# Block 0 of the output projection loaded in the last head's iteration, its units for six tiles first, and tiles turned back ahead of the next ones turned forth

## The reference

```python
h = concat(meta, x)
u = rms_norm(h, norm_mix); proj = u @ w_in
q, k, v = split(silu(causal_depthwise_conv(proj.qkv)))
o = chunk_gated_delta_rule(l2(q), l2(k), v, g, beta)     # a scan over chunks of tokens
y_a = rms(o) * head_norm * silu(z)
y_b = multiscale_causal_pool(proj.pool)
y = sigmoid(ga) * y_a + sigmoid(gb) * y_b
h = h + y @ w_out                                        # the output projection
f = rms_norm(h, norm_ffn) @ w_up; f = causal_depthwise_conv(f)
h = h + (silu(f.gate) * f.val) @ w_down
out = rms_norm(h, norm_final)[meta:]
```

## Time and profile before

| what | us |
|---|---|
| median of three runs (1749.07 to 1750.23) | 1749.51 |
| the profiled execution | 1749.15 |
| its span, first to last instruction | 1747.3 |
| PE busy in it | 1682.9 (96%) |
| DVE, ACT, POOL busy | 895.4, 609.7, 484.0 |
| mean granted clock of PE | 0.987 |

### The profile page before, as it was taken

The page is one execution under the profiler, slowest core; times in us unless marked ns, Lnnn a source line. Parts: engine busy times, 40 slices in busy tenths (PEclk is TensorE's granted clock), DMA queues, the critical chain, the costliest instruction groups (busy, mean ns, idle before and its releaser), DMA issues.

```text
span 1747.3 us, 30707 instructions
## 1 busy us (share of the span) xinstructions
PE 1682.9 (96%) x12131; PEld 1609.2 (92%) x12131; DVE 895.4 (51%) x971; ACT 609.7 (35%) x984; POOL 484.0 (28%) x469
## 2 busy tenths in 40 slices
PE   6999999997999999999789899999999999999997
PEld 6999999997999999999689898998998998989986
DVE  5566555484544454544441555545445456455447
ACT  6333465354444444443222531221212211212213
POOL 3222221136445444445011122212211221221210
PEclk9999999998999999999889999999999999999998
DMA  6223433348446445344871111111111111111112
GB/s 191 76 91 101 139 123 102 89 131 193 128 138 165 117 136 156 113 138 119 231 256 32 37 48 49 48 36 48 52 44 36 60 48 36 60 48 36 48 36 97
DMA packets 239654, 167.41 MB, mean 96 GB/s; under 512 B 43881, under 2 KB 225992, under 8 KB 238457
## 3 DMA queue, kind: packets, MB, share of 16 engines
q1 hardware_dynamic: 205492, 130.39, 26.2%
q10 hardware_dynamic: 33892, 36.28, 6.2%
q0 software_dynamic: 224, 0.12, 0.0%
HBM read 124.40 MB, written 42.37 MB: 95 GB/s over the span
## 4 chain that ended last, share of the span: by engine, by line
PE 87%; DVE 5%; DMA 2%; issue 2%; ACT 2%; POOLq 1%; DVEq 0%; POOL 0%; ACTq 0%; SPq 0%
PE gb L801 63%; PE db L1128 13%; PE db L938 4%; PE db L854 1%; PE db L1003 1%; PE db L1004 1%; DVE cacc L1604 1%; DMA ot_d<-ots 1%; DVE hx L1897 1%; PE db L1081 1%; PE db L935 1%; DVE fino L2003 1%; ACT hx L1175 0%; DVEq L1567 0%; DMA yo<-ot_d 0%
## 5 line engine op out<-in xcount | busy, mean ns | idle before, releaser
L801 PE MATMUL gb<-u_hi,w_hi 128*128 128x342 f32 (+2 forms) x2520 | 822.7, 326 | 20.3 <-ACT ht L1476 8.9
L801 PE MATMUL gb<-u_lo,w_hi 128*128 128x342 f32 (+2 forms) x2520 | 810.0, 321 | 0.0
L801 PE MATMUL gb<-u_hi,w_lo 128*128 128x342 f32 (+2 forms) x2520 | 806.8, 320 | 0.0
L688 POOL TENSOR_TENSOR w_lo<-w_raw,w_hi 128x1024 fp32r<-128x1024 f32 x127 | 322.7, 2545 | 1070.1 <-ACT w_hi L1170 1070.1
L801 PEld LDWEIGHTS gb<-u_hi,w_hi 128*128 128x128 f32 x2520 | 478.0, 190 | 24.9 <-issue 19.5
L801 PEld LDWEIGHTS gb<-u_lo,w_hi 128*128 128x128 f32 x2520 | 478.0, 190 | 0.4
L801 PEld LDWEIGHTS gb<-u_hi,w_lo 128*128 128x128 f32 x2520 | 477.4, 189 | 0.0
L1969 DVE TENSOR_TENSOR h<-h,db 128x512 f32<-128x512 f32 x176 | 117.0, 684 | 59.3 <-PE db L1128 58.8
L1128 PE MATMUL db<-w_hi,a_hi 128*128 128x512 f32 x352 | 140.9, 400 | 2.9 <-DVE a_lo L1993 2.9
L1128 PE MATMUL db<-w_lo,a_hi 128*128 128x512 f32 x352 | 139.6, 397 | 0.0
L1128 PE MATMUL db<-w_hi,a_lo 128*128 128x512 f32 x352 | 139.5, 396 | 0.0
(11 more groups left out here) (236 smaller groups left out, 1675.5 us busy)
## 6 DMA issues: line engine op xcount, KB each, us to landing
w_raw<-in_w_in SPq DMA_DIRECT2D x53, 512.0 KB, 4.0
w_raw<-in_w_up SPq DMA_DIRECT2D x44, 512.0 KB, 3.8
w_raw<-in_w_down SPq DMA_DIRECT2D x22, 512.0 KB, 3.3
qkT_d<-sl ACTq DMA_DIRECT2D x16, 576.0 KB, 2.8
kv_d<-tm ACTq DMA_DIRECT2D x16, 576.0 KB, 3.4
tk<-kv_d SPq DMA_DIRECT2D x9, 1024.0 KB, 7.7
kT<-qkT_d SPq DMA_DIRECT2D x9, 512.0 KB, 4.7
brow<-rows_d SPq DMA_DIRECT2D x9, 512.0 KB, 6.1
```

The source lines that it names most:

```text
L688: pool.tensor_tensor(lo, w_raw[:, n % SLOTS, :], hi.bitcast(F32), ALU.subtract).then_inc(s_wlo, 1)
L801: mm = pe.matmul(gb[:, bank, 0:w], wt, u, start=(k == 0 and m == 0), stop=(k == KT - 1 and m == 2))
```

## The change

Block 0 is loaded without the last head for `yz` and `yg` (7 of 8 tiles); for that head's part DVE reads the buffers `zs` and `gs` themselves. The waits of SP are loosened to match, and the tile of `ots` is put elsewhere, so that block 1's `yo` no longer waits for the write of the last OT. The weight tiles of `w_out` are loaded in the order `OUT_TILES`, tiles 0, 1 and 2 a second time. The plan begins with six tiles of block 0, with OT after two of them, then tiles 3 to 5 of blocks 1 and 2, and in its last part back stands ahead of forth. In the last down projection the first halves of eight outputs run ahead, in the four banks of `db`, three of `gb` and `mb`.

```diff
-W_UP0 = W_OUT + KT
+OUT_TILES = [0, 1, 2, 3, 4, 5, 0, 1, 2, 6, 7]
+W_UP0 = W_OUT + len(OUT_TILES)
...
-OUT_PLAN = [("unit", n, b) for b in range(3) for n in range(3)]
-OUT_PLAN += [("unit", n, b) for n in (3, 4) for b in range(3)]
-OUT_PLAN += [("unit", n, 0) for n in (5, 6, 7)]
-OUT_PLAN += [("unit", 5, 1), ("back", 0), ("unit", 6, 1), ("forth", 0), ("back", 1)]
-for _j, _unit in enumerate([("unit", 7, 1), ("unit", 5, 2), ("unit", 6, 2), ("unit", 7, 2), ("up", 0, 0),
+OUT_PLAN = [("unit", 0, 0), ("unit", 1, 0), ("OT",), ("unit", 2, 0)] + [("unit", n, b) for b in range(3) for n in (3, 4, 5)]
+OUT_PLAN += [("unit", n, b) for n, b in ((0, 1), (0, 2), (1, 1), (1, 2), (6, 0), (7, 0))]
+OUT_PLAN += [("unit", 2, 1), ("back", 0), ("unit", 6, 1), ("back", 1), ("forth", 0)]
+for _j, _unit in enumerate([("unit", 7, 1), ("unit", 2, 2), ("unit", 6, 2), ("unit", 7, 2), ("up", 0, 0),
                             ("up", 1, 0), ("up", 0, 1)]):
-    OUT_PLAN += [_unit, ("forth", _j + 1), ("back", _j + 2)]
+    OUT_PLAN += [_unit, ("back", _j + 2), ("forth", _j + 1)]
 OUT_PLAN += [("up", 1, 1), ("forth", KT), ("up", 0, 2), ("up", 1, 2)]
 OUT_UNITS = [s[1:] for s in OUT_PLAN if s[0] == "unit"]
 assert sorted(OUT_UNITS) == [(n, b) for n in range(KT) for b in range(3)]
+FIRST_OF_BLOCK = [(0, 0), (3, 1), (3, 2)]
+def out_slot(n, b):
+    return n if n in (3, 4, 5) or b == 0 and n < 3 else n + 6 if n < 3 else n + 3
+OUT_LAST = {out_slot(n, b): (n, b) for n, b in OUT_UNITS}
...
-        vv, vb, ots = plan(square_set("vv", "vb", "ots"), after_qkm)
+        vv, vb = plan(square_set("vv", "vb"), after_qkm)
+        (ots,) = plan(square_set("ots"), last_set + 4 * KT * TO)
...
+        def down_bank(u, last=False):
+            if not last or u % 8 < 4:
+                return db[:, u % 4, :]
+            return gb[:, u % 4, :] if u % 4 < 3 else mb[:, :]
...
-            for n in range(3):
-                load_w(W_OUT + n, cols(w_out, n * P))
+            def load_out(k):
+                load_w(W_OUT + k, cols(w_out, OUT_TILES[k] * P))
+            for k in range(3):
+                load_out(k)
             chunk_loads(NCH - 1, True)
...
-            def load_y(b, src, dst):
+            def load_y(b, src, dst, n=KT):
                 o, w = OBLOCKS[b]
-                sp.dma_start(dst[b % 2][:, :, :], src[:, o:o + w].rearrange("(k p) t -> p k t", p=P)
+                sp.dma_start(dst[b % 2][:, 0:n, :], src[0:n * P, o:o + w].rearrange("(k p) t -> p k t", p=P)
                              ).then_inc((s_ygin if dst is yg else s_yin)[b % 2], 16)
...
-            sp.wait_ge(s_za, 16 * HEADS)
+            sp.wait_ge(s_za, 16 * (HEADS - 1))
             sp.wait_ge(s_ps["QK"], 2 * NCH)
             sp.wait_ge(s_kg, NCH)
             sp.wait_ge(s_qd, NCH)
-            load_y(0, za_d, yz)
+            load_y(0, za_d, yz, HEADS - 1)
             sp.wait_ge(s_ev["QK"], 2 * NCH)
-            sp.wait_ge(s_ot, 16 * (NCH - 1))
+            sp.wait_ge(s_ot, 16 * (NCH - 2))
             load_y(0, ot_from, yo)
+            load_out(3)
             sp.wait_ge(s_rd, NCH)
             sp.wait_ge(s_ev["Y1"], 2 * (NCH - 1))
             sp.wait_ge(s_vb, NCH)
             sp.wait_ge(s_kd, NCH)
+            sp.wait_ge(s_yg, 16 * HEADS)
+            load_y(0, yg_d, yg, HEADS - 1)
+            load_out(4)
+            sp.wait_ge(s_ps["O"], 2 * NCH)
+            sp.wait_ge(s_za, 16 * HEADS)
+            load_y(1, za_d, yz)
             sp.wait_ge(s_yg, 16 * (HEADS + 1))
-            load_y(0, yg_d, yg)
-            sp.wait_ge(s_ps["O"], 2 * NCH)
-            load_y(1, za_d, yz)
             load_y(1, yg_d, yg)
+            load_out(5)
             sp.wait_ge(s_ps["OT"], 2 * NCH)
-            sp.wait_ge(s_ot, 16 * NCH)
             load_y(1, ot_from, yo)
-            load_w(W_OUT + 3, cols(w_out, 3 * P))
             sp.wait_ge(s_y, 2)
             load_y(2, za_d, yz)
             load_y(2, yg_d, yg)
+            sp.wait_ge(s_ot, 16 * NCH)
             load_y(2, ot_from, yo)
-            for n in (4, 5):
-                load_w(W_OUT + n, cols(w_out, n * P))
+            for k in (6, 7, 8):
+                load_out(k)
...
                 if g < 2:
-                    load_w(W_OUT + 6 + g, cols(w_out, (6 + g) * P))
+                    load_out(9 + g)
...
-            for name, prev in (("P1", LAST_Y), ("V", "P1"), ("O", "V"), ("OT", "O")):
-                step(name, NCH - 1, (prev, 2 * (NCH - 1)))
+            for name, prev in (("P1", TOP_X), ("V", LAST_Y), ("O", "P1")):
+                step(name, NCH - 1, (prev, 2 * (NCH - 2 if prev == TOP_X else NCH - 1)))
...
-                    w_ready(W_OUT + n)
+                    k = W_OUT + out_slot(n, b)
+                    w_ready(k)
                     pe.wait_ge(s_gfree, U_OUT - 3 + q + 1)
                     for hf in range(2):
-                        if n == 0:
+                        if (n, b) in FIRST_OF_BLOCK:
                             pe.wait_ge(s_y, 2 * b + hf + 1)
-                        mm = unit(W_OUT + n, q % 3, o, w, 4 * hf, 4 * hf + 4)
+                        mm = unit(k, q % 3, o, w, 4 * hf, 4 * hf + 4)
                     mm.then_inc(s_g, 1)
                     q += 1
+                elif kind == "OT":
+                    step("OT", NCH - 1, ("V", 2 * (NCH - 1)))
...
-                    mm = pe.matmul(db[:, u % 4, :], a, wt, start=(q == 0 and m == 0), stop=(q == 1 and m == 2))
+                    mm = pe.matmul(down_bank(u, n == W_LAST), a, wt, start=(q == 0 and m == 0), stop=(q == 1 and m == 2))
...
-            for u in range(4):
+            for u in range(KT):
+                if u == 4:
+                    pe.wait_ge(s_gfree, U_FFN + 12 * (FFN_ITERS - 1))
                 down_part(W_LAST, u, 0)
             for u in range(2 * KT):
                 if u % KT == 0:
                     pe.wait_ge(s_alo, FT + u // KT)
-                if u > 3:
-                    pe.wait_ge(s_dnfree, 16 * (FFN_ITERS - 1) + u - 3)
+                if u >= KT:
+                    pe.wait_ge(s_dnfree, 16 * (FFN_ITERS - 1) + u - KT + 1)
                     down_part(W_LAST, u, 0)
...
-            for name in REC:
-                act_step(name, NCH - 1)
...
+            act_step("V", NCH - 1)
             y_high(0)
+            act_step("O", NCH - 1)
+            act_step("SU", NCH - 1)
+            act.wait_ge(s_yg, 16 * (HEADS + 1))
...
-                if kind == "unit":
+                if kind == "OT":
+                    act_step("OT", NCH - 1)
...
-                    if n == 0 and b < 2:
+                    if n == 5 and b < 2:
                         y_high(b + 1)
...
-                    if b == 2:
-                        w_high(W_OUT + n + 3)
+                    if OUT_LAST[out_slot(n, b)] == (n, b):
+                        w_high(W_OUT + out_slot(n, b) + 3)
...
                 elif kind == "back":
-                    j = tile[0]
-                    n = HALO if j == 0 else P
-                    act.wait_ge(s_h2, 2 * j + 2)
...
-                    root(j, n, h2m[:, :] if j == 0 else h2[:, j - 1, :], hx[0:n, j % 2, :], s_h2sq)
+                    if tile[0] < 2:
+                        root2(tile[0])
                 else:
                     high2(tile[0])
+                    if 0 < tile[0] < KT:
+                        root2(tile[0] + 1)
...
-            def y_product(b):
+            def y_parts(b, kept, loaded):
+                o, w = OBLOCKS[b]
+                for ks in FEATURE_HALVES:
+                    if b or ks.stop < KT:
+                        yield ks, loaded[b % 2][:, ks, :]
+                    else:
+                        yield slice(ks.start, KT - 1), loaded[0][:, ks.start:KT - 1, :]
+                        yield slice(KT - 1, KT), kept[:, o:o + w].unsqueeze(1)
+            def y_low(b):
+                o, w = OBLOCKS[b]
                 s = b % 2
                 dve.wait_ge(s_yin[s], 32 * (b // 2 + 1))
...
-                    dve.tensor_tensor(yo[s][:, ks, :], yo[s][:, ks, :], yz[s][:, ks, :], ALU.mult)
-            dve_step("P1", NCH - 1, True)
-            y_product(0)
-            output_sums(NCH - 1)
-            output_scale(NCH - 1)
-            def y_low(b):
-                o, w = OBLOCKS[b]
-                s = b % 2
+                for ks, z in y_parts(b, zs, yz):
+                    dve.tensor_tensor(yo[s][:, ks, :], yo[s][:, ks, :], z, ALU.mult)
                 dve.wait_ge(s_ygin[s], 16 * (b // 2 + 1))
-                if b:
...
-                for ks in FEATURE_HALVES:
-                    dve.tensor_tensor(yo[s][:, ks, :], yo[s][:, ks, :], yg[s][:, ks, :], ALU.add).then_inc(s_y1, 1)
+                for ks, g in y_parts(b, gs, yg):
+                    t = dve.tensor_tensor(yo[s][:, ks, :], yo[s][:, ks, :], g, ALU.add)
+                    if ks.stop in (KT // 2, KT):
+                        t.then_inc(s_y1, 1)
...
-            for b in range(len(OBLOCKS)):
-                y_low(b)
+            dve_step("P1", NCH - 1, True)
```

(14 more changed lines are left out.)

17 lines of the change are left out of this document (11 added, 6 removed).

## The result

The changed kernel takes **1726.76 us** (median of four runs, 1724.27 to 1729.08) against 1749.29 (1748.84 to 1750.23): ratio 0.9875, 95% interval 0.9863 to 0.9888. The forecast was 1725.2, with a range from 1719 to 1735. Its profiled execution took 1727.12 us, span 1725.3, where the kernel before had 1747.3.

The account below looks back on a forecast made before the run. TensorE bounds the kernel nearly everywhere, so only its waits and low clock count. 19.0 - 0.9 - 0.3 + 5.0 + 1.5 = 24.3 us off 1749.15 gives 1724.9, as a median 1725.2 us, range 1719 to 1735.

Parts of the forecast that it names:

- Start of the first unit: Output projection, block 0: early loads end DVE's waits, so the first unit starts at 850.2 against 859.4.
- The clock behind that gap: Gap of 2.4 us before the first unit: a clock loss there only shortens the wait before block 2.
- Block 1: Output projection: yo lands 7.8 us after issue; PE may take the block at 874.5 to 875.3, waiting 0 to 1 us.
- Block 2 decides: Tenth unit: yo waits for OT's write, the row of loads takes 21 us, ready at 888.5; gain 19.0 us.
- The write of OT: Before block 2: earlier 11.1 us looked queued behind prior loads; by the packet-by-packet rule it would land early.
- Rival B: Before block 2: OT's write lands last, ready at 892.6, clock falls; +5, about 1730, up to 1734; chance 0.16.
- Rival A: Block 2 hidden too: loads at the full window's rate, PE waits under 1 us; about 1721; chance 0.15.
- C: Block 0's loads: held by a hidden wait, or they push bds back; at worst about 1738; chance 0.08.
- D: Gap before the first unit: clock falls and stays down, slower from 155 low matmuls on; up to 1756; chance 0.02.
- Turning phase: Back ahead of forth removes eight 0.34 us waits for hx and a low-clock unit; gain 5.0 us (2.5 to 5.4).
- a low clock behind block 2's gap: Output projection: a gap of 2.4 to 3.4 us costs 1.8 us about every second time; -0.9 (0 to 1.8).
- Last down projection: Kernel's end: 12 more matmuls fill the wait for a_lo, six behind run at full clock; gain 1.5 us (0 to 1.6).

Follow-up runs that it names:

- e6: Changed kernel, with POOL's split of the third weight tile held until DVE is through with block 0; 1725.10 us.
- e9: The changed kernel, unedited, timed and profiled a second time; 1726.05 us.
- e7: Changed kernel plus 14 idle matmuls in TensorE's gap between O and the first unit; 1724.61 us.
- e10: Changed kernel, with the sixth weight tile's load issued ahead of block 1's yz and yg instead of behind them; 1725.20 us.
- e1: Kernel before, with the new turning order alone (back ahead of forth, root and scaling placed to match); 1743.39 us.
- e2: Kernel before, with the new last down projection alone (eight first halves ahead instead of four); 1748.71 us.
- e3: Changed kernel, with turning order and last down projection put back, so the output projection's first-block change alone; 1731.65 us.
- e12: Changed kernel, with yz and yg of block 1 read from block 2's columns in memory and the reverse; 1731.41 us.
- e8: Changed kernel, with block 2's yz and yg loads held until the write of OT has landed; 1730.54 us.
- e5: Changed kernel, with the old order of three tiles per block and eight weight loads put back; 1737.14 us.

## Why the prediction was right, step by step

**Start of the first unit**: 850.2 forecast, 852.50 measured, 851.0 on the clock of the kernel before. That the loads would be there was right (DVE waits for none). The 0.8 us missing are DVE's product behind POOL's split (0.96 by e6). My price came from rows with POOL idle, and what POOL does beside them was no term of mine.

**The clock behind that gap**: I let it cost nothing, since the wait before block 2 would swallow it. The gap was 3.3 us instead of 2.4 and the first two units lost 1.6 us (2.7 in e9) against those of e7. It did pass into a later wait, as said, the one before block 1: 3.1 us in e7, 1.9 in the first profile, 0.4 in e9. But it also moved OT: PE came to it at 861.65, 1.6 us later than without the low clock (e7), and block 1's yo left as much later.

**Block 1**: "a wait of 0 to 1 us" was 1.9 and 0.4 in two profiles. The step that failed in the first is the landing time 7.8 us, which was 9.0 (7.2 in e9; 6.1 to 10.2 over all kernels): it was taken as a property of the load, and depends on how much of the row that began with block 1's yz is still under way.

**Block 2 decides**: the row of loads, 21 us from block 1's yo to block 2's, was 21.3 (862.71 to 884.0) and 19.7 in e9. That the first profile repeats the 21 us of the kernel before is luck in part: before, block 2's yo left 7.6 us behind block 1's and took 13.3; now it waited for the write of OT, left 12.7 us behind and took 8.6. Ready at 892.2 by DVE's row plus half of it, PE there at 892.5, so there was no wait to see: the forecast one of 2.4 to 3.4 us had been spent before, in front of the first unit and of block 1, together with the low clock (e9 has 0.64 us of it). Tenth unit: gain 19.0 forecast, 16.5 and 17.6 measured. The prediction's estimate by the memory limit in the Trainium skill ("DMA: Bandwidth & Descriptors", section Bandwidth) was 19.1 us for this row. The traces reach it in e10 (19.1), where the loads issued before the row had only 0.5 us left when it began, and not with more left of them: 19.7 in e9 (1.7 us left), 21.3 in the first profile (3.1), 21.8 in e7 (5.6). The limit itself, 358 GB/s, was passed a little: 364 GB/s from 864 to 880 us in the first profile.

**The write of OT**: 11.1 us again (10.4 in e9), but not as the earlier trace rows was read: it did not stand behind all that had been issued before it, and once it moved it took turns packet for packet, as the rule has it that the prediction takes from the Trainium skill ("DMA: Bandwidth & Descriptors", section Queues, rings and completion order). The row spoke against the rule only in the sum, since a start some 4 us late stands in it. Rival B came close to true in the first profile: block 2's yo left only at 875.40, when the write was in, and the block was ready at 892.2 (890.7 on the clock of the kernel before) against its 892.6; its low clock and its price of 5 us did not come, since PE was not there earlier. e9 (ready at 889.3, or 889.8 on that clock) lies nearer to the forecast 888.5. Rival A (block 2 hidden) is true in name, PE waited less than 1 us there, but the time went elsewhere. C and D fell: yz left 0.56 us behind bds, and behind the first gap some 12 matmuls ran low (20 in e9), not 155.

**Turning phase**: 5.0 forecast, 6.3 alone by the trace of e1 and 5.5 by its time. The small waits went for good. Seven of the eight cost 0.57 us, not 0.34: a forth that starts after a stop takes 1.09 us in the chain, one that runs behind back 0.87. That makes 4.3 us instead of 2.8. On the other side 1.5 us of the low clock were chance (paid in the kernel before and e2, not in e3). In the changed kernel the stage from the tenth unit on was 5.7 us shorter, and the forecast for it is 5.0 less the two terms that fall there: 0.9 for a low clock behind block 2's gap, which did not come (no gap, and 0.64 us at a granted clock of 1.00 in e9), and 0.3 for the last weight tile, which was 0.2. So 3.8 forecast.

**Last down projection**: 1.5 forecast, 1.3 by traces (1.0 to 2.2), below what the times can tell (e2).

So the sum was right within 1 us (23.5 and 24.6 for 24.3) with errors of opposite signs: 2.5 us too much to the tenth unit (1.4 in e9), 1.9 too little behind it. That they cancel is luck. What was right in the mechanism is which waits go, that the work put into them is what counts, and that block 2's last load stands behind the write; what was wrong is where PE would wait.

## What to carry to other kernels

Price a wait by what PE could do meanwhile, not only by how early its cause can be moved: the tiles put into the wait were worth 10 us, the early loads 6 to 7. Before moving one load, follow back the whole row of transfers in front of it, and ask what the second bound is, since here edits that each hit one of two gave at most 1 to 2 us at the load and nothing sure in the time. Compare short stages from a common late event: 1.5 us of difference in the spans arose more than 350 us ahead of the change.

## What the hardware showed that was not expected

**Columns of a matrix in memory load at different rates.** The same 128x8 rows of 1368 bytes, 4104 bytes apart, load at 229 GB/s from columns 342 to 683 and at 374 from 684 to 1025, in either order of time (e12), the engines full in both cases. The cause is open; yo, whose rows are farther apart (4608 bytes), loaded in company with the fast columns at 348 to 394 GB/s (windows of 2 us from 866 to 876 us in the changed kernel). Trying another row length for za and yg is the next thing to do here, and it was not done.

**POOL and DVE exclude each other, and who pays changes from profile to profile.** The changed kernel is 1.5 us late before its own change: up to 418 us it was 0.8 us early, and from that P1 to the next one, near 479, it lost 2.4. In this stretch one DVE instruction stands out; kernel before, then changed, timelines of DVE:

```profile
419.66 1.70 DVE L1673 TENSOR_TENSOR kgt<-kbt,grow 128x1024 f32<-128x1024 f32 x1
```

```profile
418.82 6.29 DVE L1711 TENSOR_TENSOR kgt<-kbt,grow 128x1024 f32<-128x1024 f32 x1
```

and the changed kernel's POOL in that stretch:

```profile
419.40 4.63 POOL L712 TENSOR_TENSOR w_lo<-w_raw,w_hi 128x1024 fp32r<-128x1024 f32 x2
```

In both kernels DVE's instruction began while POOL's product `kd` was under way (418.38 to 420.28 before, 417.55 to 419.44 after). Before, DVE got through in between, and POOL's two splits took 5.62 us. After, POOL went from `kd` into the first split and from that into the second, and DVE ended 1.1 us behind them. So in these rows DVE, though it waited, did not get in between POOL's instructions; that tenths of a microsecond decide it is my reading. PE's wait behind it was 8.10 us instead of 4.76. It is not the whole scatter: in eleven of the other twelve profiles the instruction took 1.70 us and in e8 3.00, and e2, e5 and e10, whose P1 comes as late or later (842.8 to 843.6), were late by 418 us already.

**The clock does not follow the length of the gap alone.** In the changed kernel and all that are built on it, the 4 us behind every gap of 1.82 to 12.10 us between the first unit and block 2 show a granted clock of 0.50 to 0.66, so TensorE ran at the lower of its two levels (1.2 GHz) for a part of them; behind gaps of 1.1 us and less they show 1.00. But in the turning phase a gap of 2.26 us was followed by a low unit in the kernel before (5.53 us) and in e2 (5.44), and one of 2.25 us by none in e3 (4.00). Nor does the length say for how long: behind the same 3.3 us 11 or 12 matmuls ran low in two profiles and some 20 in five.
